# Down projections with both split halves of the activations in one 512-column matmul

## The chip, the core and the metric

The kernel runs on one core of a Trainium2 chip. The metric is device time in microseconds. Three runs of the kernel before gave 1009.44 to 1010.5 us, with a median of 1009.82 us.

## The reference

The kernel computes three layers on 256 tokens of width 1024: an mLSTM layer with an MLP, a short-convolution layer with an MLP, and a third layer with retention, cross attention and a gated MLP. The change is in the MLPs of the first two layers:

```
def sqrelu_mlp(x, w_up, w_down):
    h = jax.nn.relu(x @ w_up)
    return (h * h) @ w_down

        x = x + rms_norm(h, g[1])
        h = sqrelu_mlp(rms_norm(x, g[2]), w_mlp_up[i], w_mlp_down[i])
        x = x + rms_norm(h, g[3])
```

`w_up` is 1024x4096 and `w_down` 4096x1024, all in float32. The output of the down projection is normed (`g[3]`) and added to x.

## The kernel before, in words

Activations lie transposed: 128 features on the partitions, 256 tokens (T) in the free dimension. TensorE multiplies in the format f32r, which keeps fewer bits than float32. So each operand is split in two: a high part rounded to f32r (wH, xnH, hH), and a low part, the rest (wL, xnL, hL). A product is the sum of three: wH with hH, wH with hL, wL with hH (`products`, L416 to L421). All three go to the same 256 columns of PSUM.

The weights come from HBM in slabs of 1 MB: 8 steps k of the contraction, each with two blocks n of 128 output features, so 16 blocks of 128x128 and 48 matmuls a slab. A slab goes through four buffers `raw`. ScalarE rounds it to wH (`split`, L805), VectorE subtracts to get wL (`split`, L1245), each in two halves. wH and wL have two buffers each, so the split of a half-slab waits until TensorE has finished that half two slabs before (semaphores `first_half_done` and `slab_done`).

A down projection is 16 slabs in four groups of four slabs (`mlp` on TensorE, L621 to L631). A group makes 256 output features and has one of two PSUM slots `po`, used in turn; a slot is two banks of 512 columns, one bank for each n. Before the change the first 256 columns of a bank are used. After a group ScalarE reads the slot (`keep_y`, L851): it stores the squares for the norm, then y scaled by the gain, and signals `drained_act`.

Behind the down projection the norm of y is computed (the boundary). TensorE meanwhile works on a filler: slabs of the third layer's memory projection (`fill`, L463), one behind the first MLP (f1), two behind the second (f6, f3). After two of its eight steps stand the sums of the squares (`norm_sums`, L469), which wait for the squares of all four groups. VectorE makes the mean (L1265), GpSimd the factor (L1821), VectorE a diagonal (L1271), and after the filler's step 4 TensorE spreads it to all partitions (`norm_spread`, L490). Then VectorE scales y (L1465), adds it to x, and makes with ScalarE the high and low parts of the next input (L819, L1252), for which the next phase's matmuls wait.

The order of the work on each engine is written out by hand; engines meet only at semaphores. `PHASES` lists each phase's slabs, its groups and the engine that frees its PSUM slots ("A" ScalarE, "V" VectorE); `DRAIN` counts from it what TensorE waits for.

Of the kernel before, what the change touches and what calls it, by code (L numbers as in the profile page):

```python
# [9 lines left out]
P = 128  # L25
# [26 lines left out]
    ("qk", 4, 4, "V"), ("v", 4, 4, "A"), ("o", 4, 4, "V"),  # L52
    ("out0", 4, 4, "A"), ("f4", 1, 1, "A"), ("f0", 1, 1, "V"), ("up0", 16, 16, "V"), ("down0", 16, 4, "A"), ("f1", 1, 1, "V"),
    ("cin", 12, 12, "AVV"), ("out1", 4, 4, "A"), ("f5", 1, 1, "A"), ("f2", 1, 1, "V"),
    ("up1", 16, 16, "V"), ("down1", 16, 4, "A"), ("f6", 1, 1, "A"), ("f3", 1, 1, "V"),
    ("rq", 4, 4, "V"), ("ru", 2, 2, "V"), ("rv", 2, 2, "A"), ("rg", 2, 2, "V"), ("out2", 4, 4, "V"),
# [31 lines left out]
def build(nc, xT, memT, pos, weights, wgate, params, poolw, tri, mask, select, decay, freq, recount, out):  # L88
# [4 lines left out]
    with ctx:  # L93
# [60 lines left out]
        at = [region]  # L154
        hH = sb("hH", [P, F1 // P, T], f32r, at)
        hL = sb("hL", [P, F1 // P, T], f32r, at)
        hidden_end = at[0]
# [124 lines left out]
        s_Rs = sem("R_kept")  # L282

        s_t, s_xadd, s_xaddV = sem("y_scaled"), sem("x_added_pool"), sem("x_added_dve")

# [44 lines left out]
        def slot(g):  # L330
            return po[g % 2]
# [74 lines left out]
        def _(pe):  # L406
# [9 lines left out]
            def products(psum, n, w, k, aH, aL, ac, start, stop):  # L416
# [4 lines left out]
                return pe.matmul(psum[:, n, 0:T], wL[w][:, wc], aH[:, ac, :], start=False, stop=stop)  # L421

            def slab(s, w, psum, aH, aL, c0=0, first=True, last=True, ready=None, between={}):

                for k in range(8):
                    if k % 4 == 0:
                        weights_ready(s, k // 4)
                    if ready and k % 2 == 0:
                        pe.wait_ge(ready[0], ready[1] + k // 2 + 1)
                    for n in range(2):  # L430
                        mm = products(psum, n, w, k, aH, aL, c0 + k, first and k == 0, last and k == 7)
                    if k == 3:
                        mm.then_inc(s_half, 1)
                    if k in between:
                        between[k]()
                mm.then_inc(s_slab, 1)
# [170 lines left out]
            def mlp(layer, feed, n_norm, names):  # L607
                up, down = f"up{layer}", f"down{layer}"
                s0, g0 = SLAB0[up], GROUP0[up]
                d0 = DRAIN[g0][1]  # L610

                for j in range(4):
                    phase_slab(up, j, xnH, xnL, ready=(s_xn, 4 * feed) if j == 0 else None,
                               between=norm(n_norm) if j == 1 else {})
                with pe.Fori(0, 3) as i:
                    for j in range(4):

                        pe.wait_ge(s_drain["V"], i * 4 + (d0 + 4 + j - 2))
                        slab(i * 4 + (s0 + 4 + j), (s0 + j) % HL, slot(g0 + j), xnH, xnL)

                s0, g0 = SLAB0[down], GROUP0[down]  # L621
                d0 = DRAIN[g0][1]
                with pe.Fori(0, 2) as i:
                    for j in range(2):

                        slot_free(g0 + j)
                        pe.wait_ge(s_drain["A"], i * 2 + (d0 + j - 2))
                        for kk in range(4):
                            b = s0 + 4 * j + kk
                            slab(i * 8 + b, b % HL, slot(g0 + j), hH, hL, c0=8 * kk, first=kk == 0, last=kk == 3,  # L630
                                 ready=(s_hid, 16 * layer + 4 * kk) if j == 0 else None)  # L631
                fillers(names, n_norm + 1)
# [157 lines left out]
        def _(act):  # L790
# [60 lines left out]
            def keep_y(psum, g, gain):  # L851
# [8 lines left out]
                k.then_inc(s_drain["A"], 1)  # L860

            def mix_hi(src, pair, done):
                act.wait_ge(*done)
# [121 lines left out]
            def mlp(layer, gain, n_norm):  # L985
# [23 lines left out]
                if layer == 1:  # L1009
# [4 lines left out]
                    act.wait_ge(s_trigd, 2)  # L1014
                s0 = SLAB0[down]
                with act.Fori(0, 2) as i:
                    for j in range(2):
                        for kk in range(4):
                            b = s0 + 4 * j + kk
                            split(b + 2, i, 8, halves=(0,))  # L1020
                            if kk == 3:
                                act.wait_ge(s_slab, i * 8 + (b + 1))
                                keep_y(slot(GROUP0[down] + j), i * 2 + j, gain)
                            split(b + 2, i, 8, halves=(1,))

# [203 lines left out]
        def _(dve):  # L1229
# [217 lines left out]
            def boundary(n, post, filler, feeds, gain, key):  # L1447

                nxt = SLAB0[filler] + 1
                two = nxt == SLAB0[f"f{key}"]  # L1450
                split(nxt, halves=(0,))
                mean_square(n)
                if two:
# [6 lines left out]

                dve.wait_ge(s_R, n + 1)

                def scale(p):
# [19 lines left out]
                fill_keys(key)  # L1483
                split(nxt + 2 if two else nxt + 1)

            def out_phase(name):
# [11 lines left out]
            def mlp(layer, n_norm):  # L1498
# [28 lines left out]
                for kk in range(3):  # L1527
                    split(s0 + kk + 2)
                with dve.Fori(0, 3) as i:
                    for kk in range(4):  # L1530
                        split(s0 + 3 + kk + 2, i, 4)

# [483 lines left out]
```

## Time and profile before

| | |
|---|---|
| median of the runs | 1009.82 us (1009.44 to 1010.5) |
| span of the profiled execution | 1008.9 us |
| TensorE matmul, weight load | busy 974.7 us (97%), 961.8 us (95%) |
| VectorE | 657.2 us (65%) |
| ScalarE | 536.5 us (53%) |
| GpSimd | 191.0 us (19%) |
| the two down projections | 87.22 us each |
| DMA | 172.17 MB, mean 171 GB/s |

The span runs from the first to the last instruction of the profiled execution; 0.9 us lies between it and the median of the runs. Matmuls are pipelined: a row's duration is longer than the distance to the next row's start, so the pace is read from starts. The two down projections stand from 233.93 to 321.15 us and from 537.78 to 625.00 us.

### The profile page before, as it was taken

How to read it: one execution, taken by the hardware profiler on the slowest of the kernel's cores; microseconds unless marked ns; L12 is line 12 of the kernel's file. 1: busy time of each engine (PE TensorE's matmuls, PEld its weight loads, DVE VectorE, ACT ScalarE, POOL GpSimd, SP SyncE). 2: the span in 40 equal slices, each digit the busy share in tenths (PEclk: the TensorE clock that was granted, in tenths of full speed). 3: DMA queues.
4: the chain of work that ended last, by engine and by line, in shares of the span. 5: the costliest groups of instructions: out<-in, count | busy, mean ns of one | idle time of the engine just before them, and what ended most of it. 6: DMA issues, size and time to landing. Idle time of an engine off the chain costs nothing.

```text
span 1008.9 us, 20181 instructions
## 1 busy us (share of the span) xinstructions
PE 974.7 (97%) x8062; PEld 961.8 (95%) x8062; DVE 657.2 (65%) x843; ACT 536.5 (53%) x754; POOL 191.0 (19%) x159
## 2 busy tenths in 40 slices
PE   7999989999999899999999999989999999999996
PEld 6999989999999799989999999889999999999995
DVE  6567586665444876577665444874865779999642
ACT  5566646554443544556555444554554566666541
POOL 2021140000010400149000010455120122223101
PEclk9999999999999999999999999999999999999997
DMA  9533635555555354535555553544342545555521
GB/s 342 183 126 112 216 131 188 190 171 204 186 189 172 123 206 168 189 129 190 196 173 198 182 205 137 196 159 168 128 166 86 181 152 177 197 191 183 205 88 42
DMA packets 25844, 172.17 MB, mean 171 GB/s; under 512 B 3252, under 2 KB 3892, under 8 KB 5432
## 3 DMA queue, kind: packets, MB, share of 16 engines
q1 hardware_dynamic: 25784, 171.30, 49.0%
q8 instruction: 46, 0.75, 0.3%
q14 instruction: 14, 0.11, 0.0%
HBM read 170.24 MB, written 1.05 MB: 170 GB/s over the span
## 4 chain that ended last, share of the span: by engine, by line
PE 85%; DVE 7%; issue 3%; POOL 2%; ACT 2%; DMA 1%; DVEq 0%; SPq 0%; ACTq 0%; POOLq 0%
PE po L419 25%; PE po L420 25%; PE po L421 25%; DVE xnL L1252 2%; DVE wL L1245 2%; PE po L446 2%; POOL rtok L1821 2%; PE po L448 2%; PE po L447 2%; PE pn L494 1%; ACT wH L805 1%; PE pn L487 1%; PE pc L743 1%; DMA raw<-in_weights 1%; DVE diag L1271 0%
## 5 line engine op out<-in xcount | busy, mean ns | idle before, releaser
L1245 DVE TENSOR_TENSOR wL<-raw,wH 128x1024 fp32r<-128x1024 f32 x318 | 404.0, 1294 | 157.8 <-ACT wH L805 157.8
L805 ACT ACTIVATE wH<-raw 128x1024 fp32r<-128x1024 f32 x318 | 334.8, 1059 | 295.5 <-PE po L421 264.8
L419 PE MATMUL po<-xnH,wH 128*128 128x256 f32 x1376 | 396.8, 288 | 18.9 <-DVE xnL L1252 13.2
L420 PE MATMUL po<-xnL,wH 128*128 128x256 f32 x1376 | 389.9, 283 | 0.0
L421 PE MATMUL po<-xnH,wL 128*128 128x256 f32 x1376 | 389.7, 283 | 0.0
L419 PEld LDWEIGHTS po<-xnH,wH 128*128 128x128 f32 x1376 | 264.3, 192 | 23.6 <-DVE xnL L1252 9.6
L420 PEld LDWEIGHTS po<-xnL,wH 128*128 128x128 f32 x1376 | 264.5, 192 | 0.2
L421 PEld LDWEIGHTS po<-xnH,wL 128*128 128x128 f32 x1376 | 264.4, 192 | 0.0
L419 PE MATMUL po<-hH,wH 128*128 128x256 f32 x688 | 189.9, 276 | 0.0
L420 PE MATMUL po<-hL,wH 128*128 128x256 f32 x688 | 189.9, 276 | 0.0
L421 PE MATMUL po<-hH,wL 128*128 128x256 f32 x688 | 189.9, 276 | 0.0
L1808 POOL TENSOR_TENSOR squares<-squares 128x512 f32<-128x512 f32 x26 | 39.7, 1528 | 525.0 <-ACT squares L853 368.7
L419 PEld LDWEIGHTS po<-hH,wH 128*128 128x128 f32 x688 | 129.1, 188 | 0.0
L420 PEld LDWEIGHTS po<-hL,wH 128*128 128x128 f32 x688 | 129.1, 188 | 0.0
L421 PEld LDWEIGHTS po<-hH,wL 128*128 128x128 f32 x688 | 129.1, 188 | 0.0
L419 PE MATMUL po<-mixH,wH 128*128 128x256 f32 x256 | 71.8, 280 | 0.5 <-DVE mixL L1287 0.5
L420 PE MATMUL po<-mixL,wH 128*128 128x256 f32 x256 | 71.0, 277 | 0.0
L421 PE MATMUL po<-mixH,wL 128*128 128x256 f32 x256 | 71.0, 277 | 0.0
L1512 DVE SCALAR_TENSOR_TENSOR hrelu<-po,Rs 128x512 f32<-128x512 f32 x32 | 22.1, 690 | 55.8 <-PE po L421 55.7
L1252 DVE SCALAR_TENSOR_TENSOR xnL<-x,par,xnH 128x256 fp32r<-128x256 f32 x56 | 48.6, 918 | 7.5 <-ACT xnH L819 7.5
L419 PEld LDWEIGHTS po<-mixH,wH 128*128 128x128 f32 x256 | 48.1, 188 | 0.9 <-DVE mixL L1287 0.7
L421 PEld LDWEIGHTS po<-mixH,wL 128*128 128x128 f32 x256 | 48.3, 189 | 0.0
(284 smaller groups left out, 1097.1 us busy)
## 6 DMA issues: line engine op xcount, KB each, us to landing
raw<-in_weights SPq DMA_DIRECT2D x158, 1024.0 KB, 4.8
x<-in_xT SPq DMA_DIRECT2D x4, 256.0 KB, 6.4
raw<-in_weights SPq DMA_DIRECT2D x2, 512.0 KB, 6.2
mem<-in_memT SPq DMA_DIRECT2D x1, 1024.0 KB, 12.6
out<-y SPq DMA_DIRECT2D x4, 256.0 KB, 2.4
decayt<-in_decay SPq DMA_DIRECT2D x1, 512.0 KB, 3.7
poolwt<-in_poolw SPq DMA_DIRECT2D x1, 256.0 KB, 3.7
par<-in_params SPq DMA_DIRECT2D x1, 164.0 KB, 3.4
```

What stands on the lines that cost most here:

```text
L419: pe.matmul(psum[:, n, 0:T], wH[w][:, wc], aH[:, ac, :], start=start, stop=False)
L420: pe.matmul(psum[:, n, 0:T], wH[w][:, wc], aL[:, ac, :], start=False, stop=False)
L421: return pe.matmul(psum[:, n, 0:T], wL[w][:, wc], aH[:, ac, :], start=False, stop=stop)
L446: pe.matmul(psum[:, t, 0:256], aH[:, k, tc], wH[w][:, wc], start=k == 0, stop=False)
L447: pe.matmul(psum[:, t, 0:256], aL[:, k, tc], wH[w][:, wc], start=False, stop=False)
L448: mm = pe.matmul(psum[:, t, 0:256], aH[:, k, tc], wL[w][:, wc], start=False, stop=k == 7)
L805: act.activation(wH[b % HL][:, hs], raw[b % RAW][:, hs], ACT.Copy).then_inc(s_hi, 1)
L1245: dve.tensor_tensor(wL[b % HL][:, hs], raw[b % RAW][:, hs], wH[b % HL][:, hs].bitcast(f32), ALU.subtract)\
L1252: k = dve.scalar_tensor_tensor(xnL[:, c, :], x[:, c, :], col(gain, c), xnH[:, c, :].bitcast(f32), ALU.mult, ALU.subtract)
L1512: dve.scalar_tensor_tensor(hrelu[n % 2][:, :, :], slot(GROUP0[up] + n)[:, :, 0:T], 0.0, over_pair(Rs[:, :]), ALU.max, ALU.mult).then_inc(s ...
L1808: pool.tensor_tensor(sq[0], sq[0], sq[p], ALU.add).then_inc(s_sqa, 1)
L1821: pool.tensor_tensor(r[:, :], ms[:, :], minus_half[:, 0:TT], ALU.pow).then_inc(s_r, 1)
```

## The change

For the down projections of the two MLPs, hH and hL become the two halves of one tensor hX. `wide_products` issues one matmul of 512 columns for both halves past wH. The bank's first 256 columns then hold hH with wH, and the last 256 hold hL with wH. The product of wL with hH is added to the first 256 as before. So a group ends with two sums, and the drain joins them: ScalarE copies the low sum to y (`keep_low_part`), VectorE adds the other (`add_parts`) and frees the slot, ScalarE squares y and scales it in place (`gain_y`). The loops of ScalarE and VectorE over the groups are written out. VectorE waits for `y_gained` before it scales y at the boundary.

```
-    ("out0", 4, 4, "A"), ("f4", 1, 1, "A"), ("f0", 1, 1, "V"), ("up0", 16, 16, "V"), ("down0", 16, 4, "A"), ("f1", 1, 1, "V"),
+    ("out0", 4, 4, "A"), ("f4", 1, 1, "A"), ("f0", 1, 1, "V"), ("up0", 16, 16, "V"), ("down0", 16, 4, "V"), ("f1", 1, 1, "V"),
...
-        hH = sb("hH", [P, F1 // P, T], f32r, at)
-        hL = sb("hL", [P, F1 // P, T], f32r, at)
+        hX = sb("hX", [P, 2, F1 // P, T], f32r, at)
+        hH, hL = hX[:, 0, :, :], hX[:, 1, :, :]
...
+            def wide_products(psum, n, w, k, aX, ac, start, stop):
+
+                wc = slice(k * 256 + n * P, k * 256 + (n + 1) * P)
+                pe.matmul(psum[:, n, :].rearrange("p (a t) -> p a t", a=2), wH[w][:, wc], aX[:, :, ac, :], start=start, stop=False)
+                return pe.matmul(psum[:, n, 0:T], wL[w][:, wc], aX[:, 0, ac, :], start=False, stop=stop)
...
-                        mm = products(psum, n, w, k, aH, aL, c0 + k, first and k == 0, last and k == 7)
+                        if aL is None:
+                            mm = wide_products(psum, n, w, k, aH, c0 + k, first and k == 0, last and k == 7)
+                        else:
+                            mm = products(psum, n, w, k, aH, aL, c0 + k, first and k == 0, last and k == 7)
...
+            def keep_low_part(name, g, layer):
+
+                act.wait_ge(s_slab, SLAB0[name] + 4 * g + 4)
+                act.activation(y[:, 2 * g:2 * g + 2, :], slot(GROUP0[name] + g)[:, :, T:2 * T], ACT.Copy).then_inc(s_ylo, 1)
+
+            def gain_y(name, g, gain, layer):
+                act.wait_ge(s_drain["V"], DRAIN[GROUP0[name] + g][1])
+                act.activation(squares[:, g, :, :], y[:, 2 * g:2 * g + 2, :], ACT.Square).then_inc(s_sq, 1)
+                act.wait_ge(s_sq, 4 * (4 * layer + 4) + g + 1)
+                for e in range(2):
+                    dst = y[:, 2 * g + e, :]
+                    k = act.activation(dst, dst, ACT.Identity, scale=col(gain, 2 * g + e))
+                k.then_inc(s_ygain, 1)
...
-                with act.Fori(0, 2) as i:
-                    for j in range(2):
-                        for kk in range(4):
-                            b = s0 + 4 * j + kk
-                            split(b + 2, i, 8, halves=(0,))
-                            if kk == 3:
-                                act.wait_ge(s_slab, i * 8 + (b + 1))
-                                keep_y(slot(GROUP0[down] + j), i * 2 + j, gain)
-                            split(b + 2, i, 8, halves=(1,))
+                for j in range(4):
+                    for kk in range(3):
+                        split(SLAB0[down] + 4 * j + kk + 2)
+                    split(SLAB0[down] + 4 * j + 5, halves=(0,))
+                    keep_low_part(down, j, layer)
+                    split(SLAB0[down] + 4 * j + 5, halves=(1,))
+                    gain_y(down, j, gain, layer)
...
+                if post % 2:
+                    add_parts(f"down{post // 2}", 3, post // 2)
                 mean_square(n)
...
+                if post % 2:
+                    dve.wait_ge(s_ygain, 2 * post + 2)
...
+            def add_parts(name, g, layer):
+                dve.wait_ge(s_ylo, 4 * layer + g + 1)
+                ys = y[:, 2 * g:2 * g + 2, :]
+                dve.tensor_tensor(ys, ys, slot(GROUP0[name] + g)[:, :, 0:T], ALU.add).then_inc(s_drain["V"], 1)
```

On TensorE, at the start of the first down projection, the rows of before are (wH_53 and wL_55 are the buffers of the high and low weights, hH and hL the split activations):

```order
L627 ISA [waits drained_dve]
L408 ISA [waits drained_act]
L419 MATMUL po<-hH,wH_53 128x256 [waits hidden_ready,weights_lo]
L420 MATMUL po<-hL,wH_53 128x256
L421 MATMUL po<-hH,wL_55 128x256
```

At the same place in the changed kernel:

```order
L622 ISA [waits drained_dve]
L394 ISA [waits drained_dve]
L412 MATMUL po<-hX,wH_53 128x512 [waits hidden_ready,weights_lo]
L413 MATMUL po<-hX,wL_55 128x256
L412 MATMUL po<-hX,wH_53 128x512
```

Two matmuls stand where three stood, and the slot's wait is for VectorE alone.

On ScalarE, at the end of the first down projection, the rows of before from the split of the filler's first half-slab on (wH_54 is a weight buffer):

```order
L805 ACTIVATE wH_54<-raw_52 128x1024 [waits first_half_done]
L853 ISA [waits slab_done]
L853 ACTIVATE squares<-po 128x512
L859 ISA
L859 REGISTER_ALU
L859 ACTIVATE y<-po,par 128x256
L859 ISA
L859 REGISTER_ALU
L859 ACTIVATE y<-po,par 128x256
L805 ACTIVATE wH_54<-raw_52 128x1024 [waits slab_done,raw_loaded3]
```

And in the changed kernel:

```order
L800 ACTIVATE wH_54<-raw_52 128x1024 [waits first_half_done,raw_loaded3]
L860 ACTIVATE y<-po 128x512 [waits slab_done]
L800 ACTIVATE wH_54<-raw_52 128x1024 [waits slab_done,raw_loaded3]
L864 ACTIVATE squares<-y 128x512 [waits drained_dve]
L868 ACTIVATE y<-y,par 128x256 [waits squares]
L868 ACTIVATE y<-y,par 128x256
```

The squares were the first operation after the group's end. Now they stand third, behind the copy of the low sum and the split of a half-slab, and wait for VectorE.

## Rows read from the trace of the kernel before

**Rows 1.** The page's first part: busy time, share of the span, instructions.

```profile
PE 974.7 (97%) x8062; PEld 961.8 (95%) x8062; DVE 657.2 (65%) x843; ACT 536.5 (53%) x754; POOL 191.0 (19%) x159
```

**Rows 2.** The page's fourth part: the chain that ended last, by engine.

```profile
PE 85%; DVE 7%; issue 3%; POOL 2%; ACT 2%; DMA 1%; DVEq 0%; SPq 0%; ACTq 0%; POOLq 0%
```

**Rows 3.** Busy time by windows, both down projections; clock, DMA share, GB/s last.

```profile
core 0: us, PE busy (x) PEld busy (x) DVE busy (x) ACT busy (x) POOL busy (x), PEclk, DMA share, GB/s
233.93:321.15 87.22, 87.22 (x772) 87.22 (x771) 41.78 (x35) 38.81 (x43) 3.33 (x3) 1.00 0.57 195
537.78:625.00 87.22, 87.22 (x772) 87.22 (x771) 41.70 (x35) 40.70 (x46) 3.34 (x3) 1.00 0.51 177
```

**Rows 4.** Timeline of TensorE inside a down projection (start us, us, what).

```profile
239.73 0.28 PE L419 MATMUL po<-hH,wH 128*128 128x256 f32 x1
...
242.90 0.28 PE L420 MATMUL po<-hL,wH 128*128 128x256 f32 x1
```

**Rows 5.** Chain of work, an fp32 product of the cross attention (start, us, what).

```profile
767.13 1.73 PE pc L743 x8
```

**Rows 6.** Timeline of the weight loads around one-column matmuls of the retention.

```profile
707.03 1.87 PEld L683 LDWEIGHTS pn<-ones,rosq 128*128 128x128 f32 x16
708.82 0.19 PEld L419 LDWEIGHTS po<-xnH,wH 128*128 128x128 f32 x1
```

**Rows 7.** Timeline of TensorE inside the first up projection.

```profile
149.72 0.28 PE L421 MATMUL po<-xnH,wL 128*128 128x256 f32 x1
...
150.80 0.28 PE L421 MATMUL po<-xnH,wL 128*128 128x256 f32 x1
```

**Rows 8.** End of the first down projection: chain on TensorE, timeline of ScalarE.

```profile
321.15 0.12 PE po L419
322.57 1.23 PE pn L487 x12
321.29 0.60 ACT L853 ACTIVATE squares<-po 128x512 f32 x1 [1.76 <-PE po L421]
321.79 0.83 ACT L859 ACTIVATE y<-po,par 128x256 f32 x2
322.50 1.06 ACT L805 ACTIVATE wH<-raw 128x1024 fp32r<-128x1024 f32 x1
328.82 0.61 ACT L822 ACTIVATE squares<-x 128x512 f32<-128x512 f32 x1
```

**Rows 9.** VectorE's adds with a PSUM operand (L1669): duration min/median/max.

```profile
L1669 DVE TENSOR_TENSOR x<-x,po x8: 679/687/689, 722.0 to 806.9; 128x512 f32<-128x512 f32 x8
```

**Rows 10.** Timeline: one half-slab's split on ScalarE and VectorE in the down projection.

```profile
315.81 1.06 ACT L805 ACTIVATE wH<-raw 128x1024 fp32r<-128x1024 f32 x1 [1.72 <-PE po L421]
316.90 1.23 DVE L1245 TENSOR_TENSOR wL<-raw,wH 128x1024 fp32r<-128x1024 f32 x1 [1.56 <-ACT wH L805]
```

**Rows 11.** Chain of work: the norm's spread in the stream, and after a wait.

```profile
326.07 0.46 PE pn L494 x4
630.13 0.71 PE pn L494 x4
```

**Rows 12.** Timeline of TensorE: idle time ahead of the next phase's matmuls.

```profile
330.73 0.35 PE L419 MATMUL po<-xnH,wH 128*128 128x256 f32 x1 [2.07 <-DVE xnL L1252]
641.51 0.39 PE L419 MATMUL po<-xnH,wH 128*128 128x256 f32 x1 [1.31 <-DVE xnL L1252]
```

## Prediction of the time after the change

> **What bounds the kernel now.** I read the page first. In its table of busy time [rows 1] the reader sees TensorE busy for 97% of the span and its weight loads for 95%; VectorE and ScalarE have a third and almost a half of the span free. The chain that ended last [rows 2] says the same in another way: 85% of it is TensorE, 7% VectorE. So a microsecond taken from TensorE's stream counts in full, unless it stands at a place where TensorE waits. Then the stretches by time: the two down projections [rows 3] take 87.22 us each, TensorE is busy in all of it, at full granted clock (1.00, the 2.4 GHz level), VectorE for 41.8 us and ScalarE for 39 to 41 us, and DMA at 0.51 to 0.57. Nothing feeds TensorE late there, and the stream itself sets the time. Last the single matmuls in order of time [rows 4]: 28 starts take 242.90 - 239.73 = 3.17 us, 0.113 us each. Taken over the stretch, 768 matmuls (16 slabs of 48) in 87.22 us are 0.1136 us each, and a triple, which is one 128x128 block with its three products, takes 0.3407 us.
>
> **What the slot of 113.6 ns is made of.** 256 columns at the granted clock of 2.4 GHz are 106.7 ns. The other 6.9 ns are what this change can win, and the question is to what they belong. Three rows bear on it.
> First, fp32 matmuls of 256 columns [rows 5] take 1.73 us for eight records, 0.2163 us each. Their slot is about twice ours, so they stream for 512 cycles (213.3 ns) and pay 3.0 ns over that, with a weight load of the same 128x128 beside every one.
> Second, matmuls with one column [rows 6] are pure weight loads: 16 loads start between 707.03 and 708.82, which is 0.112 us each although almost nothing is streamed. A weight load alone needs 112 ns, more than our 106.7 ns of streaming.
> Third, the products with xn take 0.120 us a slot [rows 7] (nine starts in 150.80 - 149.72 = 1.08 us) with the same shape, clock and count of columns as the products with h. A pace that varies by 6 ns with the tile is not that of streamed columns alone.
> I read these together: a slot of 256 columns is set by the weight load of the next block, and a slot of 512 columns by its columns. Where a load hides below 512 cycles it costs 3 ns.
> The Trainium skill bears on this at "TensorE: Matmul & The Clock Gate", section "LDWEIGHTS (loading the stationary operand)": a load takes its columns divided by 1.2 GHz, an estimate of 106.7 ns, just the time of our 256 columns. By that the load would not be the longer of the two. Rows 6 show 112 ns, and by the trace it is.
>
> **The change part by part.**
> *Removed:* per block and slab, two matmuls of 256 columns with a load each (hH and hL past wH). *Added:* one matmul of 512 columns with one load. The third (wL with hH) stays. There are 16 slabs x 16 blocks x 2 layers = 512 triples. The last down projection (fdown) has the same tiles but keeps its three matmuls, so nothing is counted for it. No row shows an f32r matmul of 512 columns. Its bounds: at best it takes 0.2163 us as in rows 5 and the narrow one falls to its own streaming plus the same 3 ns, 0.1097 us, together 0.3260 (14.7 ns less, 7.5 us in all). At worst the whole excess goes with the columns: 2 x 0.1136 + 0.1136 = 0.3407, nothing won. I take the nearest row for each: 0.2163 for the wide one (512 cycles with a load of 128x128 beside it), and 0.1136 for the narrow one, below which the next high load must still be done. That is 0.3299, 10.8 ns less, and 512 x 10.8 ns = **5.5 us won**.
> *The sum of a group is split in two.* ScalarE's read of the group's sum (squares from po 0.60 us, two scalings 0.83 us [rows 8]) becomes: ScalarE copies the low half to y, VectorE adds the high half and thereby frees the PSUM slot, ScalarE squares y and scales it in place. Per group that is one more ScalarE operation of 0.60 us and one more of VectorE with a PSUM operand, 0.69 us [rows 9]; eight groups, so 4.8 and 5.5 us on engines that have over 45 us free in a stretch of 87. A slot is wanted again only after the next group, four slabs or 21 us later. The work for the weights has room too: in [rows 10] the high half of a weight half-slab starts at 315.81 and its low half ends at 316.90 + 1.23 = 318.13, while TensorE comes to it a slab and a half after it freed the buffer (8.2 us after 315.7, near 323.9): 5.8 us of slack. What ScalarE and VectorE do between two slabs grows by about 1.3 us. I cost all groups but the last at nothing. Were that cover gone, it would be up to 1.3 us for each of the six inner groups.
> *The last group of each layer is not covered.* Behind it TensorE computes two of eight steps of the filler (12 matmuls) and then the sums of squares, which wait for the squares of the last group. Before, from the end of the last product at 321.15 (T) the squares are done at T + 0.74 and TensorE arrives at T + 1.42 (322.57), so nobody waits [rows 8]. Now the copy runs T + 0.14 to T + 0.74. ScalarE then has a weight split of 1.06 us ahead of the squares, which by the overlap of 0.10 us seen between its operations ends at T + 1.70. VectorE's add (T + 0.77 to T + 1.46) is done by then, so the split and not the add holds the squares back: T + 1.60 to T + 2.21, as squares from SBUF take 0.61 us [rows 8]. TensorE waits 0.80 us. It also restarts empty: two small matmul groups of one form take 0.46 us in the stream and 0.71 us after a wait [rows 11], 0.25 us more. Queued behind the waiting sums on TensorE are six steps of the filler and the spread of the norm, for which VectorE waits, and with it the residual, the split of xn and the next phase. Both boundaries have idle TensorE later on that waits for this very chain (2.07 us ahead of 330.73, 1.31 ahead of 641.51 [rows 12]), so none of the delay is absorbed: it moves the chain, and the idle time moves with it. 2 x 1.05 = **2.1 us lost**. Bounds: nothing, if the squares came in time as before; 1.5 us each, if the add is late by a further semaphore or two.
> *The gained y* is waited for by VectorE ahead of the scaling. It is done 0.9 us after the squares, while the norm's factor takes over 3 us: no cost.
>
> **The sum.** -5.5 + 2.1 = -3.4 us on the profiled execution. Its span is 1008.9 us and the median of the runs 1009.8, so 0.9 us lies around the span and is carried over unchanged. 1009.8 - 3.4 = **1006.4 us**. A difference of 0.2% (2.0 us) is about what a measurement of this kernel can tell from no change.
>
> **The rivals.**
> *A, the narrow slot shrinks as well.* If two loads can run ahead below the wide matmul, the narrow slot is 0.1097: 7.5 - 2.1 = 5.4 us faster, 1004.4. Against it stands that rows 6 show loads one after the other at 112 ns with an idle array, with nothing to show one queued further ahead. 10%.
> *B, the excess of 6.9 ns belongs to every matmul, whatever its width.* Then one of three goes: 512 x 6.9 ns = 3.5 us, less 2.1, 1008.4. For it: it is the simplest reading of the slots with h. Against it: rows 5 pay 3.0 and not 6.9. 10%.
> *C, only a small fixed cost belongs to the matmul* and the rest to the columns: of the 6.9 ns, 3.0 (rows 5) are fixed and 3.9 come per 256 columns. The wide one takes 213.3 + 7.8 + 3.0 = 224.1 ns, the triple 337.7, and 512 x 3.0 ns = 1.5 us are won, 2.1 lost: 1010.4. f32r reads a new element in each cycle, and the fp32 of rows 5 only in every second, so a read limit would not show in rows 5. Against it stand rows 6 and 7. 8%. The Trainium skill says much the same in "TensorE: Matmul & The Clock Gate", "Back-to-back issue gap": a warm gap is N/2.4 ns plus about 2.5 ns. By that a merge saves 2.5 ns, an estimate of 1.3 us in all. The trace has 113.6 ns where the rule gives 109.2, so it lacks what I hold to be the weight load.
> *D, slower: the pace is that of the columns,* 0.444 ns each at any width, as a limit on reading f32r from SBUF would make it. The wide matmul takes 227 ns or more, nothing is won, and the two waits remain: + 2.1 to + 3.0, about 1012.3. It decides from a wide slot of 0.227 us on. For it: nothing in the trace streams f32r wider than 256. Against it: two loads out of three then go for nothing although rows 6 show them to be longer than the columns. 10%.
> *E, it doesn't do what it says,* and the wide matmul runs as two passes, each with its load: the time of D. 2%, since it is one instruction with one load.
>
> **How the numbers follow.** My forecast has 60%, with its own range 1005.3 to 1007.6 (the waits between 0.5 and 1.5 us each, the wide slot within 1.5 ns). A 10, B 10, C 8, D and E 12. The range reaches over A, B and C: 1004.0 to 1010.8, which leaves D, E and a little beside A out. Faster by over 0.2% (below 1007.8): the forecast and A, 0.70. Within: B and C, 0.18. Slower (above 1011.8): D and E, 0.12.
>
> **What would show it.** The h rows of the changed kernel: 512 wide matmuls and 512 fewer loads; starts 0.216 us after a wide one and 0.113 us after a narrow one; down stretches of 84.5 us in place of 87.22 (rival A 83.5, B 85.4, C 86.4, D 87.2). At each layer's end the first matmul of the sums of squares about 1 us later after the last product than before, with the squares of y as what it waited for and a weight split ahead of these on ScalarE. I am wrong if the down stretches stay above 86 us, if TensorE waits inside them (for a slot or for weights), or if the waits at the two ends pass 1.5 us.

## The result, and the profile after

The changed kernel takes 1020.5 us in the median (1018.5 to 1022.2, four runs), the kernel before, run beside it, 1010.2 us (1009.4 to 1012.3, four runs). The ratio is 1.010, with a 95% interval of 1.0083 to 1.0116. So the change costs 1.0%, where I forecast 0.3% less time; 1020.5 lies outside the range of 1004.0 to 1010.8.

The first part and the fourth part (the chain) of the page after, with the two groups of the new products from its fifth:

```profile
PE 982.3 (96%) x7550; PEld 945.3 (93%) x7550; DVE 661.5 (65%) x851; ACT 541.4 (53%) x762; POOL 198.6 (20%) x159
PE 85%; DVE 7%; issue 3%; POOL 2%; ACT 2%; DMA 1%; DVEq 0%; SPq 0%; ACTq 0%; POOLq 0%
L412 PE MATMUL po<-hX,wH 128*128 128x512 f32 x512 | 181.0, 397 | 0.0
L413 PE MATMUL po<-hX,wL 128*128 128x256 f32 x512 | 143.9, 281 | 0.0
```

Against [rows 1] there are 512 matmuls and 512 weight loads fewer, as the change says, and yet TensorE is busy for 7.6 us more. The chain has the same shares as in [rows 2]: TensorE's stream still sets the time. The two down projections by windows, beside [rows 3]:

```profile
core 0: us, PE busy (x) PEld busy (x) DVE busy (x) ACT busy (x) POOL busy (x), PEclk, DMA share, GB/s
235.71:326.33 90.62, 90.62 (x516) 78.75 (x515) 43.62 (x38) 40.55 (x46) 5.42 (x3) 1.00 0.53 189
542.71:633.32 90.61, 90.61 (x516) 78.68 (x515) 43.60 (x38) 42.56 (x49) 5.42 (x3) 1.00 0.48 171
```

They grew by 3.40 and 3.39 us at the same clock, with TensorE never idle. 256 pairs in 90.61 us are 353.9 ns a pair, where three narrow matmuls took 340.7. The timeline of TensorE in the stretch shows how a pair is divided (start us, us, what):

```profile
253.38 0.40 PE L412 MATMUL po<-hX,wH 128*128 128x512 f32 x1
253.61 0.28 PE L413 MATMUL po<-hX,wL 128*128 128x256 f32 x1
253.73 0.40 PE L412 MATMUL po<-hX,wH 128*128 128x512 f32 x1
...
254.79 0.40 PE L412 MATMUL po<-hX,wH 128*128 128x512 f32 x1
```

The narrow one starts 0.23 us after the wide one (235.0 ns in the mean of all 512), the next wide one 0.12 us later (118.3 ns). Together that is 353.3, against 340.1 for three narrow ones by their starts; the 0.6 ns up to 353.9 and 340.7 are the end of the stretch's last matmul, shared out. I had given them 216.3 and 113.6. Then the end of the first down projection, the timeline of TensorE, ScalarE and VectorE, beside [rows 8]:

```profile
326.05 0.28 PE L413 MATMUL po<-hX,wL 128*128 128x256 f32 x1
...
326.36 0.60 ACT L860 ACTIVATE y<-po 128x512 f32<-128x512 f32 x1 [1.70 <-PE po L413]
...
326.86 1.05 ACT L800 ACTIVATE wH<-raw 128x1024 fp32r<-128x1024 f32 x1
...
326.99 0.69 DVE L1500 TENSOR_TENSOR y<-y,po 128x512 f32<-128x512 f32 x1 [1.08 <-ACT y L860]
...
327.81 0.61 ACT L864 ACTIVATE squares<-y 128x512 f32<-128x512 f32 x1
...
328.57 1.47 PE L482 MATMUL pn<-ones,squares 128*128 128x1 f32 x12 [0.81 <-ACT squares L864]
```

The last product ends at 326.33. The split stands between the copy and the squares, and the sums of squares start 2.24 us after the last product where they started 1.42 us after it before. TensorE waits 0.81 us. The first products of the next phase start at 336.97 in place of 330.73, 6.24 us later, while the stretch ended 5.18 us later: 1.06 us were added here and none of it was absorbed. The second end reads the same (a wait of 0.82 us ahead of 635.56).

The span grew by 9.3 us (1008.9 to 1018.2): 6.8 in the two stretches, 2 x 1.06 at their ends, and 0.4 elsewhere. That rest is a sum of shifts of both signs in parts which the change doesn't touch, up to 1.3 us each. The largest: around 337 us of the kernel before, products with xn start 0.21 us apart, at the 1.2 GHz level (granted clock 0.50 from 336.2 to 339.3 us), and after they don't; against it, by windows, the span's start (15 to 18 us) had a granted clock of 1.00 before and 0.51 after, which put TensorE 1.1 us back, and 192 products ahead of the first up projection took 117.0 ns each after and 113.5 before, 0.7 us in all (the last section comes back to this).

### The profile page after: what moved, and what is told of

Its sections match the earlier page's. It is cut to its first block, busy times and chain, and to the rows that moved or that the text cites. A ratio compares the mean times of both kernels' runs of the same rounds, so it can differ in the third digit from the quotient of the medians.

```text
span 1018.2 us, 19087 instructions
## 1 busy us (share of the span) xinstructions
PE 982.3 (96%) x7550; PEld 945.3 (93%) x7550; DVE 661.5 (65%) x851; ACT 541.4 (53%) x762; POOL 198.6 (20%) x159
## 4 chain that ended last, share of the span: by engine, by line
PE 85%; DVE 7%; issue 3%; POOL 2%; ACT 2%; DMA 1%; DVEq 0%; SPq 0%; ACTq 0%; POOLq 0%
PE po L405 19%; PE po L407 19%; PE po L406 19%; PE po L412 12%; PE po L413 6%; DVE xnL L1258 2%; DVE wL L1251 2%; PE po L441 2%; POOL rtok L1840 2%; PE po L443 2%; PE po L442 2%; ACT wH L800 1%; PE pn L489 1%; PE pn L482 1%; PE pc L738 1%
## 5 line engine op out<-in xcount | busy, mean ns | idle before, releaser
L1251 DVE TENSOR_TENSOR wL<-raw,wH 128x1024 fp32r<-128x1024 f32 x318 | 398.5, 1276 | 154.7 <-ACT wH L800 154.5
L405 PE MATMUL po<-xnH,wH 128*128 128x256 f32 x1376 | 396.8, 288 | 18.7 <-DVE xnL L1258 13.2
L412 PE MATMUL po<-hX,wH 128*128 128x512 f32 x512 | 181.0, 397 | 0.0
L1827 POOL TENSOR_TENSOR squares<-squares 128x512 f32<-128x512 f32 x26 | 41.8, 1607 | 532.1 <-ACT squares L864 276.4
L413 PE MATMUL po<-hX,wL 128*128 128x256 f32 x512 | 143.9, 281 | 0.0
L412 PEld LDWEIGHTS po<-hX,wH 128*128 128x128 f32 x512 | 96.3, 188 | 23.7
L413 PEld LDWEIGHTS po<-hX,wL 128*128 128x128 f32 x512 | 96.1, 188 | 0.0
L405 PE MATMUL po<-hX,wH 128*128 128x256 f32 x176 | 48.6, 276 | 0.0
L406 PE MATMUL po<-hX,wH 128*128 128x256 f32 x176 | 48.6, 276 | 0.0
L407 PE MATMUL po<-hX,wL 128*128 128x256 f32 x176 | 48.6, 276 | 0.0
## 6 DMA issues: line engine op xcount, KB each, us to landing
mem<-in_memT SPq DMA_DIRECT2D x1, 1024.0 KB, 13.2
```

Source lines behind the costliest of these rows:

```text
L405: pe.matmul(psum[:, n, 0:T], wH[w][:, wc], aH[:, ac, :], start=start, stop=False)
L406: pe.matmul(psum[:, n, 0:T], wH[w][:, wc], aL[:, ac, :], start=False, stop=False)
L412: pe.matmul(psum[:, n, :].rearrange("p (a t) -> p a t", a=2), wH[w][:, wc], aX[:, :, ac, :], start=start, stop=False)
L413: return pe.matmul(psum[:, n, 0:T], wL[w][:, wc], aX[:, 0, ac, :], start=False, stop=stop)
L1251: dve.tensor_tensor(wL[b % HL][:, hs], raw[b % RAW][:, hs], wH[b % HL][:, hs].bitcast(f32), ALU.subtract)\
L1827: pool.tensor_tensor(sq[0], sq[0], sq[p], ALU.add).then_inc(s_sqa, 1)
```

## Experiments

All times are of the slowest core; ratios are against the kernel before, run on the same chip.

**Three narrow matmuls, two sums.** The wide product is issued as two, and everything else of the change stays.

```
-  pe.matmul(psum[:, n, :].rearrange("p (a t) -> p a t", a=2), wH[w][:, wc], aX[:, :, ac, :], start=start, stop=False)
+  pe.matmul(psum[:, n, 0:T], wH[w][:, wc], aX[:, 0, ac, :], start=start, stop=False)
+  pe.matmul(psum[:, n, T:2 * T], wH[w][:, wc], aX[:, 1, ac, :], start=False, stop=False)
```

> The changed kernel, but the wide matmul is issued as two of 256 columns, each with its own weight load; where the sums lie in PSUM and how they are drained stay as changed. Theory 1 (a column of an f32r matmul costs the same at any width, and what made the columns dearer, 0.460 ns in place of 0.444, is the wide form itself): the down stretches return to 87.2 us, slots 113.6 ns, and only the two waits of 1.06 us remain, so 1012.3 us. Theory 2 (the columns grew dearer because half of the results go to the other half of the bank): the stretches stay near 90.6 us, 1019 to 1020 us. Theory 3 (weight loads set the slot, as I forecast): three loads again, also 87.2 us; it differs from theory 1 only in the widths measured apart.

Measured: 1013.9 us (8 runs), ratio 1.0021 (1.0010 to 1.0031). Its down projections by windows:

```profile
234.43:321.65 87.22, 87.22 (x772) 87.22 (x771) 43.62 (x38) 40.55 (x46) 5.42 (x3) 1.00 0.56 195
538.02:625.24 87.22, 87.22 (x772) 87.22 (x771) 43.54 (x38) 42.53 (x49) 5.42 (x3) 1.00 0.51 177
```

The stretches are back at 87.22 us to the last digit, with the second sum, the copy and the add in place. So the 6.8 us come from the wide form of the matmul alone. What is left over the kernel before, 0.21% or 2.1 us (interval 1.0 to 3.1), is what my sum gave the two waits.

**The wide product's columns in one piece.** The tile of activations holds the halves of a chunk side by side, so that 512 columns are read in one run instead of two.

```
-        hX = sb("hX", [P, 2, F1 // P, T], f32r, at)
+        hX = sb("hX", [P, F1 // P, 2, T], f32r, at)
```

> The changed kernel with hX laid out so that the high and low half of a chunk lie side by side: the wide matmul reads 512 neighbouring columns instead of two pieces of 256 that lie 32 KB apart. Theory 1 (the two pieces cost the extra 8 ns of a wide matmul): wide slot 227 ns or less, down stretch 87.2 us or less, total 1012 to 1013 us. Theory 2 (columns are as dear in any layout when wide and narrow alternate): wide slot 235 ns, stretch 90.6 us, total 1020 us. My forecast's own value for the wide slot, 216 ns, would give 84.5 us a stretch and 1006 to 1007 us.

Measured: 1021.3 us (4 runs), ratio 1.0098 (1.0076 to 1.0120), and by windows a first down projection of

```profile
234.28:324.89 90.61, 90.61 (x516) 78.75 (x515) 43.62 (x38) 40.55 (x46) 5.42 (x3) 1.00 0.53 188
```

The same 90.61 us. The jump of the pattern in the middle of the read costs nothing.

**The way out of the sums alone.** All three products go into one sum, as before, and the copy and the add of the change are kept. As there is no second sum, the copy reads the same columns as the add.

```
-    slab(i * 8 + b, b % HL, slot(g0 + j), hX, None, c0=8 * kk, ...
+    slab(i * 8 + b, b % HL, slot(g0 + j), hH, hL, c0=8 * kk, ...
```

> The matmuls of the kernel before (three of 256 columns into one sum), with the drain of the changed kernel. The copy reads the same sum that is then added to it, so y comes out doubled ahead of its norm. If the two waits at the layers' ends are the whole price of the new drain, the down stretches take 87.2 us, the first matmul of the sums of squares starts 1.0 to 1.1 us later behind each, and the total is 1012.2 us, 2.1 over before. If the longer work of ScalarE and VectorE between slabs also counts, the stretches are longer than 87.2. If idle time further on takes up the waits, the total is that of before.

Measured: 1014.9 us (7 runs), ratio 1.0032 (1.0020 to 1.0043). By windows, and the wait at the first end on the timeline of TensorE:

```profile
234.67:321.90 87.23, 87.23 (x772) 87.23 (x771) 43.62 (x38) 40.55 (x46) 5.42 (x3) 1.00 0.56 195
```

```profile
324.13 1.47 PE L482 MATMUL pn<-ones,squares 128*128 128x1 f32 x12 [0.82 <-ACT squares L864]
```

The six inner groups cost nothing, and the wait is the changed kernel's. This part of the sum stands.

**Slots by width and tile.** Behind the end of the changed kernel, series of 24 matmuls, each kind twice. The very first series ran at the 1.2 GHz level (0.213 us a slot for h 256), so its kind counts from its second pass alone.

> The changed kernel with series of 24 matmuls each behind its end, when all other engines are done, every series twice. They measure a slot by itself: f32r moving columns 128, 256, 384, 512 in one piece, 512 in two pieces, wide and narrow in turn, three narrow ones in two sums, moving tile xn in place of h, and the stationary block taken from xn or h in place of the weights. If columns set the pace: 0.443 ns or more per column at every width from 256 on, 227 ns or more at 512. If weight loads set it (my forecast): 112 to 114 ns at 128 and 256, near 163 at 384, 216 at 512. If the address of the moving tile decides between 113 and 120 ns, xn takes 120 whatever it streams past and h 113. If it is the distance or conflict between moving and stationary tile, h past xn and xn past h change places.

Rows of the chain of waits in the second pass (start us, us, what), in order h 256, h 384, h 512 in one piece, h 512 in two, h 128, xn 256, xn 512:

```profile
1073.97 2.84 PE po L800 x24
...
1077.14 4.26 PE po L803 x24
...
1081.75 5.71 PE po L806 x24
...
1087.80 5.71 PE po L809 x24
...
1101.70 2.74 PE po L821 x24
...
1104.83 2.98 PE po L824 x24
...
1108.15 5.59 PE po L827 x24
```

A row holds 0.06 to 0.12 us for the first load, which nothing hides; from start to start within a series, its first few left out, the slots are:

| columns past a 128x128 block | h (ns) | xn (ns) |
|---|---|---|
| 128 | 111.6 | |
| 256 | 113.4 | 120.0 |
| 384 | 173.4 | 173.4 (next experiment) |
| 512 | 233.5 | 228.2 |
| 512 and 256 in turn | 235 + 118 | |
| 256, three in two sums | 113.4 | |

The whole loss is here, outside the kernel's dataflow: no wait, DMA or other engine is needed for it. 128 columns cost almost what 256 do, and from 256 on each further 128 of h cost 60 ns, more than the 53.3 ns they are at 2.4 GHz. With xn they don't: its slot of 512 columns starts at 224 to 236 ns and settles at 226.7 after ten matmuls, so that 256, 384 and 512 columns take 120.0, 173.4 and 226.7 ns, each 13.3 ns over the streaming time. Further series: h past blocks of xn 117.7, xn past blocks of h 117.8, h past blocks of h 119.8 ns for 256 columns.

**Blocks of 64 columns, and more widths.** If the weight load sets the slot of 256 columns, a block half as wide must shorten it.

> Series of 24 matmuls behind the end of the changed kernel again, each twice. Blocks of 64 stationary columns in place of 128 halve the weight load and leave the moving columns. If columns set the slot from 256 on and loads only below: h 128 past 64 falls from 112 ns to some 57 to 60, h 256 past 64 stays at 113, h 512 past 64 stays at 233. If loads set the slot of 256, it falls to 107 to 110 with blocks of 64. If the load running beside the stream is what makes columns dear, h 512 past 64 is shorter than 233. Widths 320 and 448 should lie on the line of 256, 384 and 512 (0.469 ns per further column): 143 and 203 ns. xn 384 by its own line between 120 and 228: 174. fp32 at 512: twice 429 ns. mem 512 as xn 512, 228.

The chain's rows, in order: 256 columns past 128, and past a block of 64; 512 past 64; 128 past 64; fp32 with 512 columns:

```profile
1086.20 2.85 PE po L800 x24
...
1089.39 2.90 PE po L803 x24
...
1092.63 5.64 PE po L806 x24
...
1098.61 1.50 PE po L809 x24
...
1129.56 20.71 PE po L830 x48
```

With a block of 64, 128 columns fall from 111.6 to 60.0 ns, but 256 don't fall: they take 119.0 where they took 113.4 past a block of 128, more and not the same as I had expected, and no run shows why. 512 stay at 232.7. So the load sets the slot at 128 columns and not at 256, and my reading of [rows 6] was wrong. The fp32 product takes 429.2 ns for each of the 48 records that its 24 matmuls leave, 1024 cycles (426.7 ns) and 2.5 ns. Other series of the run: 320 columns 146.5, 448 columns 202, xn with 384 173.4, mem with 512 227.8 ns (settled at 226.7, as xn), one block of weights past another 120.0 with 256 columns.

**The norm's squares ahead of the second split.** In the changed kernel, ScalarE's squares are put ahead of the second half-slab's split.

```
-                    split(SLAB0[down] + 4 * j + 5, halves=(1,))
                     ...
+                    split(SLAB0[down] + 4 * j + 5, halves=(1,))
```

> The changed kernel with the squares and the gain of a group ahead of the split of the second half-slab on ScalarE. In the changed kernel the copy ends 0.63 us after the last product, and the split keeps ScalarE until 1.6 us. If the split alone held the squares, they start at about 0.7 us and TensorE's wait of 0.81 us goes. By my sum the add (over at 1.36 us) comes right behind: the squares start 1.4 us after the last product instead of 1.5, and TensorE waits 0.7 us of its 0.8. Total 1020 us either way within noise; only the rows of the boundary count.

Measured, in one run: 1020.1 us, a span of 1017.9. The timeline at the first end:

```profile
324.87 0.60 ACT L860 ACTIVATE y<-po 128x512 f32<-128x512 f32 x1 [1.70 <-PE po L413]
325.51 0.69 DVE L1500 TENSOR_TENSOR y<-y,po 128x512 f32<-128x512 f32 x1 [1.08 <-ACT y L860]
326.23 0.63 ACT L864 ACTIVATE squares<-y 128x512 f32<-128x512 f32 x1 [0.75 <-DVE y L1500]
...
327.00 1.47 PE L482 MATMUL pn<-ones,squares 128*128 128x1 f32 x12 [0.74 <-ACT squares L864]
```

TensorE waits 0.74 us in place of 0.81: with the split gone from the way, the add stands right behind it. The wait is the price of three operations in a row, not of the split's place.

**Another place for the tiles of xn.** h past weights takes 113, xn past the same weights 120 ns. In the kernel before (without the change), the four tiles xnH, xnL, memH, memL are allocated behind the scratch area, at an offset within a KB like that of the tiles of h.

> The kernel before, with xnH, xnL, memH and memL allocated behind the scratch area instead of ahead of it, from about 142 KB on in each partition, next to hH and hL; the weights stay at 48 to 80 KB. Nothing else moves. The products with xn and mem take 120.0 ns a slot before, those with h 113.4. Theory 1 (the address of the moving tile against that of the stationary one decides): xn falls to 113 to 118 ns, 4400 products with xn or mem save 2 to 6.6 ns each, 9 to 29 us less in all. Theory 2 (it is not the address but the phase, or what the other engines do in these phases): xn stays at 120 ns and the total at 1010 us.

Measured: 997.2 us (4 runs), ratio 0.9844 (0.9811 to 0.9878). The four runs lie far apart (993.6 to 1001.7 us). In the page's fifth part the xn products (before: 389.7 us, 283 ns each in the same group), and by windows the first and the second up projection, each with the down projection behind it:

```profile
L421 PE MATMUL po<-xnH,wL 128*128 128x256 f32 x1376 | 385.0, 280 | 0.0
```

```profile
152.00:227.00 75.00, 75.00 (x664) 75.00 (x664) 50.44 (x57) 47.16 (x58) 0.00 (x0) 1.00 0.56 197
227.50:314.50 87.00, 87.00 (x770) 87.00 (x769) 41.78 (x35) 38.80 (x43) 3.33 (x3) 1.00 0.56 196
448.00:526.00 78.00, 78.00 (x665) 78.00 (x664) 53.27 (x57) 46.78 (x58) 22.34 (x20) 1.00 0.55 191
526.10:616.50 90.40, 90.40 (x770) 90.40 (x769) 41.73 (x35) 40.64 (x46) 3.33 (x3) 1.00 0.49 172
```

Not a single instruction was changed, and 1.6% of the time went. The windows tell another thing. From start to start both kinds take 113.3 ns in the first two of them and 117.8 in the last two: here the h products ran at 118 ns in their second down projection, with the code and the tiles that gave 113.4 before.

**Moving tile at 18 to 208 KB.** Whether the distance to the weights in SBUF decides.

> The kernel before, and behind its end series of 24 f32r matmuls of 256 columns, each twice, whose moving tile (8 KB) lies at 18, 28, 39, 96, 112, 120, 128, 138, 148, 176 or 208 KB of each partition, once past the weights at 48 to 64 KB and once past blocks at 208 KB. So far: xn at 88 KB past the weights 120 ns, h from 157 KB on 113 to 118, xn moved to 142 KB 113 to 118. Theory 1 (two halves, with the edge at 128 KB): past the weights 120 ns up to 120 KB and 113 to 118 from 128 KB on; past 208 KB the other way round. Theory 2 (distance decides, some 60 KB or more): past the weights the step lies between 96 and 112 KB, and past 208 KB between 138 and 148. Theory 3 (only the moving tile's own address counts): the same step in both sets, in the same direction.

Chain rows, two of the places, one past weights and one past blocks that lie at 208 KB:

```profile
1101.87 2.96 PE po L808 x24
...
1141.44 2.98 PE po L844 x24
```

All places gave 118.4 or 118.8 ns past the weights and 119.7 to 119.9 past the blocks. All these tiles start at a multiple of 1 KB. The place in KB doesn't matter; each theory that I had put down fell.

**Offset within a KB alone.** In the kernel before, the small tensors (5568 bytes) are allocated ahead of xnH instead of behind memv. xn moves by these bytes only, from about 88 to 94 KB, and starts at 576 instead of 128 within a KB; so do memH and memL, and memk and memv move by as much.

```
-        xnH = sb("xnH", [P, C, T], f32r)
-        ...
         (the small tensors)
+        xnH = sb("xnH", [P, C, T], f32r)
+        ...
```

> The kernel before, with the small tensors (identity, ones, parameters and so on, 5568 bytes) allocated ahead of xnH and not behind memv. xnH, xnL, memH and memL then start at 576 bytes past a multiple of 1 KB, as hH and hL do, and not at 128, as the weights do; they stay in the lower half, at 94 KB, and everything behind the small tensors stays where it was. The series by place showed that a tile's distance in KB does nothing. Theory 1 (what counts is where moving and stationary tile start within a line or bank pattern of at most 1 KB): xn runs at 113 to 118 ns as in the run that moved it behind the scratch area, total 994 to 1001 us. Theory 2 (the run that moved it gained for another reason): xn stays at 120 ns, total 1010 us.

Measured: 997.2 us (4 runs from 993.5 to 1005.8), ratio 0.9882 (0.9825 to 0.9939). The xn group, and the first up projection by windows:

```profile
L421 PE MATMUL po<-xnH,wL 128*128 128x256 f32 x1376 | 383.4, 279 | 0.0
```

```profile
150.83:228.31 77.48, 77.48 (x684) 77.48 (x684) 51.50 (x59) 48.27 (x60) 0.00 (x0) 1.00 0.55 193
```

From start to start that is 113.5 ns. The same stretch before:

```profile
152.00:233.00 81.00, 81.00 (x678) 81.00 (x677) 51.48 (x59) 48.24 (x60) 0.00 (x0) 1.00 0.54 183
```

Here it is 120.0 ns. With the place ruled out by the series above, the offset brings the gain, and this is, with the one above, the fastest version of all: both are ahead of the kernel before and of the changed one.

**Which offset.** Series with the moving tile at offsets from 0 to 960 bytes over a KB, past weights that start at 128 modulo 256.

> The kernel before, and behind its end series of 24 f32r matmuls past the weights, whose moving tile starts at 160 KB plus an offset from 0 to 960 bytes (20 offsets): 256 columns, 512 columns, and the two in turn; all twice. Theory 1 (weight load and moving stream collide in SBUF depending on their offsets): the slot of 256 runs between 112 and 120 ns by offset, with a period of 128 bytes or more, and 512 between 216 and 235. If some offset gives 216 for the wide one beside 113 for the narrow one, the forecast 330 ns a pair is to be had there, and the change loses only by where hX lies. Theory 2 (columns of f32r cost 0.44 ns or more anywhere): no offset gives a wide slot under 227 ns or a pair under 340.

Chain rows at 32 bytes (512 columns; 512 and 256 in turn), then at 128 bytes:

```profile
1321.74 5.72 PE po L832 x24
...
1327.80 4.27 PE po L835 x24
...
1377.70 5.59 PE po L868 x24
...
1383.63 4.35 PE po L871 x24
```

For the offsets taken beyond 256 bytes, all multiples of 64, the slots repeat with a period of 256 bytes (ns):

| offset modulo 256 | 256 columns | 512 columns | pair in turn |
|---|---|---|---|
| 0 | 118.4 | 232.1 | 351.1 |
| 32 | 117.4 | 234.4 | 346.5 |
| 64 | 117.8 | 233.3 | 353.3 |
| 128 (as the weights) | 119.8 | 228.1 | 353.3 |
| 192 | 117.8 | 228.9 | 348.9 |

16, 32, 48 and 96 were taken once each, with 116.7 to 119.0 ns for 256 columns. No offset gives a wide slot under 228 in the mean of a series (at 128 it settles at 226.7) or a pair under 346 ns, against 340.7 for three narrow ones at 113.6. So none of these places of the tile saves the change.

## Why the prediction was wrong

**The failed step** is "I take the nearest row for each: 0.2163 for the wide one (512 cycles with a load of 128x128 beside it), and 0.1136 for the narrow one". Measured: 235.0 and 118.3 ns (353.9 a pair over the stretch, to be set against the forecast 329.9). In place of 10.8 ns won a triple, 13.2 ns were lost, and 512 x 13.2 ns are 6.8 us lost in place of 5.5 won. The three-narrow experiment puts all of this on the wide form, and the series show it with nothing else around. So the wide slot was taken too small by 18.7 ns and the narrow one beside it by 4.7.

*Why [rows 5] were the wrong neighbour.* A record of an fp32 matmul of 256 columns (each leaves two) and an f32r matmul of 512 both stream for 512 cycles. But the fp32 record spends two cycles a column and its slot is hardly longer than that (216.3 of 213.3 ns; 429.2 of 426.7 at 512 columns), while the f32r one has a new column each cycle and takes 227 to 235. Under rival C I had named a limit on reading new columns as the reason. That is not shown: no run tells whether fp32 reads a column once for two cycles or twice. Shown is that its row doesn't stand for f32r of the same cycles, and I took it by its cycles.

*What the 6.9 ns over the streaming time are.* I gave them to the weight load. With blocks of 64 the load is clearly shorter (60 ns a slot at 128 columns) and the slot of 256 columns is not (119.0 ns). The load of 112 ns is only the bound for 128 columns. For h the excess comes with the columns: 6.7 ns at 256, 13.4 at 384, 20 at 512 and 22 in the changed kernel. For xn it is 13.3 ns at each of these widths. That [rows 7] show 120 ns for xn was a fact about offsets (below), and I used it as an argument for the load.

*The rivals.* D was the right kind, a pace of the columns at any width, and gave 1012.3, since it costed the wide matmul at two narrow ones (227 ns). The rest, 8 ns, and the 5 ns by which the narrow slot stood higher beside it, were in none of my cases. Whether the wide neighbour does that isn't settled: 118.3 is found in all six wide stretches of three kernels and in the series in turn, where h alone took 113.4; but series of 256 columns alone at the same distance in offset took 117.8 in another run. A, B and C all needed a slot that is partly fixed per matmul, which the series show for xn and not for h. Such a rule stands in the Trainium skill too ("TensorE: Matmul & The Clock Gate", "Back-to-back issue gap": columns divided by 2.4 GHz and 2.5 ns more). For fp32, taken by cycles, the runs agree to 0.5 ns; for f32r they have 113.4 to 120.0 where it gives 109.2, and 227 to 235 where it gives 215.8. E fell: there are 512 wide matmuls with one load each, and three loads for a block became two.

**What was right.** *The ends of the layers:* forecast 0.80 us of waiting and 0.25 for the restart, held by the squares behind a split, nothing absorbed; measured 0.81 and 0.82, with a shift of 1.06 each. The two experiments that keep only this part give 2.1 us (interval 1.0 to 3.1) and 3.2 us (2.0 to 4.3). *Inner groups:* forecast free, and the stretches of both stay at 87.22 and 87.23. *The price of the split's place:* by my sum the add would be done 0.24 us ahead of it, so moving the split could win at most little; 0.07 us was won.

**The range.** The bounds of the wide slot were 326.0 and 340.7 ns for a triple. The upper one, "the whole excess goes with the columns", took for granted that twice the columns cost at most twice the time and that the narrow slot stays where it was. Neither was shown by a row.

## What to carry to other kernels

A merge of two matmuls into one of twice the width saves a weight load, but what it saves of the slot has to be measured for the very tiles. Two slots of h (226.8 ns) became 233.5 to 235; two of xn (240.0) became 228 in the series, 12 ns less, though no kernel was run with them merged; and at 128 columns, where the load is the longer, two slots of h (223.2) became 113.4. Where the trace has no row of the new width in the same type, a series of two dozen matmuls behind the kernel's end gives the slot in one run, and it should be taken in the order in which the kernel will issue them: the series in turn gave the kernel's 235 and 118 ns, the series apart 233.5 and 113.4. And a sum that gains one more engine on its way out costs only where the next consumer waits for the last one, there in full.

## What the hardware showed that I had not expected

*The pace of f32r columns has several levels at full clock.* 256 columns took 113.4, 117.8 or 120.0 ns a matmul in the kernels. Moving and stationary tile at the same offset modulo 256 bytes always gave 119.3 to 120.0 (xn, h past h and one block of weights past another in the series, the 128-byte row of the table), and xn left that level by a change of allocation alone: its groups fell from 283 ns in the mean to 280 and 279. From start to start the 4128 products with xn took 12.9 and 17.2 us less in the two profiled executions, those with h 5.9 and 2.5 us more, and the spans fell by 9.6 and 16.2 us. At other offsets kernels show 113 or 118, and the series 113.4 to 119.0. The Trainium skill ("TensorE: Matmul & The Clock Gate", "Step-by-step: what each phase is for") says that streaming and weight load have independent read ports. That the slot hangs on how the two tiles lie to each other speaks for something that they share all the same; what it is, no run here shows.

*What chooses between 113 and 118 stays open.* The same code and tiles gave 113.4 in a down projection of one kernel and 118 in that of another. In the two kernels with xn moved, a level holds as long as the stream isn't interrupted (but for its first 25 or so products), even from one tile to the next: their six down projections, the last one included, run at the level of the xn products just ahead of them, at 113, 118 and 118 in the one and 113, 113 and 118 in the other. It changes where something stood in between: a wait, the norm's matmuls, or no more than one late start. One such place is the timeline of TensorE in the first up projection of the kernel with the xn tiles moved by the small tensors:

```profile
151.96 0.28 PE L421 MATMUL po<-xnH,wL 128*128 128x256 f32 x1
152.08 0.33 PE L419 MATMUL po<-xnH,wH 128*128 128x256 f32 x1
152.25 0.28 PE L420 MATMUL po<-xnL,wH 128*128 128x256 f32 x1
...
152.72 0.28 PE L421 MATMUL po<-xnH,wL 128*128 128x256 f32 x1
152.83 0.28 PE L419 MATMUL po<-xnH,wH 128*128 128x256 f32 x1
...
153.97 0.28 PE L420 MATMUL po<-xnL,wH 128*128 128x256 f32 x1
```

Up to 152.08 the starts are 0.12 us apart, the next comes 0.17 us later, and from 152.72 on eleven starts take 1.25 us, 0.1136 each. In the other kernel the start at 447.17 us comes 0.21 us behind the one before, and 113 becomes 118 there; at the same point of this one (446.54 us) as late a start leaves it at 113. A small hiccup in the stream thus seems to be enough to shift it to another level, though not each one does it. This was only seen, not made to happen. By these rows a down projection of 768 products at 118 in place of 113 ns is 3.4 us longer, 0.3% of the kernel, without any change in its code. That may be why the runs of these two kernels lie 8 and 12 us apart, but only one execution of each was profiled.
